# Keeping x transposed through a two-layer hybrid encoder: model dimension on partitions

## The reference

```python
h = rms_norm(x, norm_mix[l])                 # x * rsqrt(mean(x*x) + eps) * gain
proj = h @ w_in[l]                           # 2048 -> 4096, split among four mixers
ya, yb, yc, yd = fourier_mix(..), s5_mix(..), attention_mix(..), rwkv7_mix(..)   # 512 wide each
ycat = rms_norm(stack(ya, yb, yc, yd), branch_norm[l])
x = x + ycat @ w_out[l]                      # 2048 -> 2048
x = x + peer_ffn(rms_norm(x, norm_ffn[l]), peer_w_query[l], peer_sub_keys[l], peer_u[l], peer_v[l])
```

## Time and profile before

| | |
|---|---|
| median of 3 executions | 4031.67 us (4027.1 to 4036.65) |
| the profiled execution | 4039.34 us, its span 4037.5 us |
| mean granted PE clock | 0.971 |
| PE busy | 3754.7 us (93%) |
| PEld busy | 3402.6 us (84%) |
| DVE busy | 2310.8 us (57%) |
| ACT busy | 429.9 us (11%) |
| bytes moved | 1077.47 MB, 267 GB/s over the span |

### The profile page before, as it was taken

One profiled execution on the slowest core, in us unless ns is written; L12 is line 12 of the kernel. 1 busy time (PEld: TensorE's weight loads), 2 busy tenths in 40 slices (PEclk: granted clock), 3 DMA queues, 4 the chain that ended last, 5 costly groups with the idle time before them and its releaser, 6 DMA issues. The chain is left out here.

```text
span 4037.5 us, 63918 instructions
## 1 busy us (share of the span) xinstructions
PE 3754.7 (93%) x26660; PEld 3402.6 (84%) x26660; DVE 2310.8 (57%) x4099; ACT 429.9 (11%) x1020; POOL 977.3 (24%) x868
## 2 busy tenths in 40 slices
PE   6997889999999999999869978899999999999997
PEld 5776774899999999999857867748999999999997
DVE  6975752695287534344469757527952875444444
ACT  1013220100111000000010132101001110000000
POOL 2510000034033333333226100000340333333331
PEclk9998899999999999999989988999999999999999
DMA  5340014399799999999744300153997999999997
GB/s 155 117 133 10 1 43 155 123 358 402 277 381 381 414 416 414 415 412 415 317 127 132 118 10 1 43 161 126 369 409 282 380 386 412 415 415 415 412 414 305
DMA packets 334771, 1077.47 MB, mean 267 GB/s; under 512 B 52197, under 2 KB 150873, under 8 KB 268441
## 3 DMA queue, kind: packets, MB, share of 16 engines
q1 hardware_dynamic: 223896, 670.72, 43.8%
q0 software_dynamic: 110592, 402.70, 25.2%
HBM read 1071.23 MB, written 2.10 MB: 266 GB/s over the span
## 5 line engine op out<-in xcount | busy, mean ns | idle before, releaser
L1745 PE MATMUL bank<-ex_W,ex_tile 128*128 128x160 f32 x8192 | 1132.6, 300 | 39.1 <-DMA ex_tile<-in_peer_v 38.8
L1745 PEld LDWEIGHTS bank<-ex_W,ex_tile 128*128 128x128 f32 x8192 | 1114.9, 190 | 60.3 <-DMA ex_tile<-in_peer_v 52.9
L1672 PE MATMUL bank<-ycT,ex_tile 128*128 128x160 f32 x8192 | 1142.8, 300 | 24.0 <-DMA ex_tile<-in_peer_uT 21.7
L1672 PEld LDWEIGHTS bank<-ycT,ex_tile 128*128 128x128 f32 x8192 | 1119.3, 190 | 39.9 <-DMA ex_tile<-in_peer_uT 30.5
L1629 POOL DMA_INDIRECT ex_row<-in_peer_u,ex_rows x384 | 404.1, 1052 | 1850.9 <-DVE ex_rows L1905 1188.7
L1941 DVE SCALAR_TENSOR_TENSOR ex_sums<-ex_row,ex_weight,ex_sums 128x2048 f32<-128x2048 f32 x186 | 437.0, 2349 | 411.4 <-DMA ex_row<-in_peer_v,ex_rows 362.3
L1935 DVE CUSTOM_DVE_ANT_0 ex_row<-ex_row,ex_h_wide 128x2048 f32<-128x2048 f32 x192 | 438.7, 2290 | 366.7 <-DMA ex_row<-in_peer_u,ex_rows 288.9
L1629 POOL DMA_INDIRECT ex_row<-in_peer_v,ex_rows x384 | 364.7, 950 | 890.2 <-DVE ex_sums L1941 560.5
L359 PE MATMUL pj_bank<-pj_hT,pj_piece 128*128 128x256 f32 x2048 | 459.5, 383 | 5.9 <-DVE pj_hT L632 3.6
L359 PEld LDWEIGHTS pj_bank<-pj_hT,pj_piece 128*128 128x128 f32 x2048 | 388.4, 192 | 72.0 <-issue 13.8
L824 PE MATMUL bank<-arena,ycT 128*128 128x512 f32 x512 | 222.4, 593 | 2.0 <-PEq L909 2.0
(11 more groups left out here) (375 smaller groups left out, 3129.3 us busy)
## 6 DMA issues: line engine op xcount, KB each, us to landing
ex_tile<-in_peer_uT SPq DMA_DIRECT2D x256, 1024.0 KB
ex_tile<-in_peer_v SPq DMA_DIRECT2D x256, 1024.0 KB
pj_piece<-in_w_in SPq DMA_DIRECT2D x32, 2048.0 KB, 8.8
arena<-in_w_out SPq DMA_DIRECT2D x16, 2048.0 KB, 8.2
query_w<-in_peer_w_query SPq DMA_DIRECT2D x16, 1024.0 KB, 6.0
ex_row<-in_peer_u,ex_rows POOLq DMA_INDIRECT x384
ex_row<-in_peer_v,ex_rows POOLq DMA_INDIRECT x384
x<-in_x SPq DMA_DIRECT2D x1, 2048.0 KB, 8.8
```

What stands on the lines that cost most here:

```text
L1672: mm = mmul(o, ring[:, j % SLOTS, k * P:k * P + P], hT[k // 4][:, k % 4, 0:DENSE], start=(k == 0), stop=(k == KT - 1))
L1745: mm = mmul(bank[:, at_, lo:lo + DENSE], ring[:, i % SLOTS, m * P:m * P + P], W[:, j, :], start=(j == 0 and m % 3 == 0), stop=(j == TILES ...
```

## The change

x stays `[P, KT, SEQ]`, dimension on partitions, from the input to the output; the host hands it in transposed and transposes the result.

- Front of mixers: ACT squares x in four quarters; PE multiplies them with a matrix of ones (16 calls of 256 columns into one bank), which leaves each token's sum on every partition; ACT takes the root of 128x256, DVE inverts it and forms hT with 16 products of x, gain and 1/rms. No transposes of h. s5_w_glu has a place of its own. PE waits for hT tile by tile in the first two parts.
- Output projection: w_out is the weight and ycT streams: 32 calls of 256 columns a piece.
- route: no turns. hT is x times gain from SBUF, after the last piece; squares of all 16 tiles are kept and summed by 16 calls with ones, 12 ahead of the 12 query calls and 4 behind them; root and reciprocal are 128x256; PE turns two tiles of it for the column that the scores need.
- experts: hT is scaled by the wide 1/rms from SBUF. A fold is 16 calls with the sums as weights and the 0/1 matrix streaming 32 columns, and one add. At the end DVE adds the six banks straight to x, then the fold of set 2; no copies, no turns back.

The diff, cut to its core:

```diff
-        x = sb(whole, "x", [P, TB, D])
+        x = sb(whole, "x", [P, KT, SEQ])
...
-                for b in range(TB):
...
-                    pe.wait_ge(h_ready, b + 1)
-                    for k in range(KT):
-                        if b == 1 and k == 12:
-                            pe.wait_ge(cols_ready, 2)
-                        mm = tr(bank[:, 4 * b + k // 4, k % 4 * P:k % 4 * P + P], h[:, k * P:k * P + P], c("ident"))
-                        if k % 4 == 3:
-                            mm.then_inc(hT_mm, 1)
-                pe.wait_ge(hT_ready, 8)
+                for q in range(4):
+                    pe.wait_ge(sq_x, q + 1)
+                    for m in range(4):
+                        mm = mmul(bank[:, 4, 0:SEQ], c("ones"), work[:, q, m * SEQ:m * SEQ + SEQ], start=(q == 0 and m == 0),
+                                  stop=(q == 3 and m == 3))
+                mm.then_inc(sums_mm, 1)
...
+                            if part < 2:
+                                pe.wait_ge(hT_ready, k + 1)
...
-                for b in range(TB):
-                    do(A.activation(work[:, 0:2, :].rearrange("p a n -> p (a n)"), x[:, b, :], ACT.Square,
-                                    accum_out=ssq[:, b:b + 1]))
-                    do(A.activation(ssq[:, 2 + b:3 + b], ssq[:, b:b + 1], ACT.Sqrt, scale=1.0 / D, bias=c("eps")), rms_ready)
+                for q in range(4):
+                    do(A.activation(work[:, q, :].rearrange("p (k s) -> p k s", k=4), x[:, 4 * q:4 * q + 4, :], ACT.Square),
+                       sq_x, wait=False)
+                act.wait_ge(sums_mm, 1)
+                do(A.activation(rstd[:], bank[:, 4, 0:SEQ], ACT.Sqrt, scale=1.0 / D, bias=c("eps")), rms_ready)
...
-                for b in range(TB):
-                    dve.wait_ge(rms_ready, b + 1)
-                    do(V.reciprocal(ssq[:, 4 + b:5 + b], ssq[:, 2 + b:3 + b]))
-                    if b:
-                        dve.wait_ge(hT_mm, 4)
-                    do(V.tensor_scalar(h[:], x[:, b, :], ssq[:, 4 + b:5 + b], None, ALU.mult), h_ready)
...
-                for b in range(TB):
-                    for q in range(4):
-                        dve.wait_ge(hT_mm, 4 * b + q + 1)
-                        do(V.tensor_tensor(hT[:, 4 * q:4 * q + 4, b * P:b * P + P],
-                                           bank[:, 4 * b + q, :].rearrange("p (k s) -> p k s", k=4),
-                                           col("norm_mix", 4 * q, 4).unsqueeze(2).to_broadcast([P, 4, P]), ALU.mult),
-                           hT_ready, wait=False)
+                dve.wait_ge(rms_ready, 1)
+                do(V.reciprocal(rstd[:], rstd[:]), rstd_ready)
+                for k in range(KT):
+                    do(V.scalar_tensor_tensor(hT[:, k, :], x[:, k, :], col("norm_mix", k), rstd[:], ALU.mult, ALU.mult),
+                       hT_ready, wait=False)
...
-        b, k = divmod(j, HALF_K)
-        mm = nc.tensor.matmul(bank[:, out_bank(n) + b, :], ycT[:, kh * HALF_K + k, b * P:b * P + P], out_w["place"][:, i % 2, k, :],
-                              start=(kh == 0 and k == 0), stop=(kh == 1 and k == HALF_K - 1), skip_group_check=True)
-    if last == TB * HALF_K:
+        m, k = divmod(j, HALF_K)
+        mm = nc.tensor.matmul(bank[:, out_bank(n) + m // 2, m % 2 * SEQ:m % 2 * SEQ + SEQ],
+                              out_w["place"][:, i % 2, k, m * P:m * P + P], ycT[:, kh * HALF_K + k, :],
+                              start=(kh == 0 and k == 0 and m % 2 == 0), stop=(kh == 1 and k == HALF_K - 1),
+                              skip_group_check=True)
...
+                tr, mmul = nc.tensor.transpose, nc.tensor.matmul
+
+                def sums(first, last):
+                    for k in range(first, last):
+                        if k % 2 == 0:
+                            pe.wait_ge(squared, k // 2 + 1)
+                        mm = mmul(bank[:, 7, 0:SEQ], c("ones"), squares[:, k, :], start=(k == 0), stop=(k == KT - 1),
+                                  skip_group_check=True)
+                    if last == KT:
+                        mm.then_inc(sums_mm, 1)

                 for i in range(EARLY, len(OUT_PIECES)):
                     if i == len(OUT_PIECES) - 2:
-
...
-                    if i == len(OUT_PIECES) - 1:
-                        pe.wait_ge(sk_out, 2)
-                        turn(0)
-                        turn(1)
-                    out_products(nc, out_w, bank, pe, ycT, i, 0, TB * HALF_K)
-                turn(2)
+                    out_products(nc, out_w, bank, pe, ycT, i, 0, OUT_MM)
+                pe.wait_ge(sk_out, 2)
+                sums(0, 12)
                 pe.wait_ge(query["w_in"][0], 16)
-                pe.wait_ge(hT_ready, 2)
-                query_products(nc, query, bank, hT, 0, 0, 8)
-                turn(3)
                 pe.wait_ge(hT_ready, 3)
-                query_products(nc, query, bank, hT, 0, 8, 12)
+                query_products(nc, query, bank, hT, 0, 0, 12)
+                sums(12, KT)
+                pe.wait_ge(rstd_ready, 1)
+                for b in range(TB):
+                    mm = tr(bank[:, 6, b * P:b * P + P], rstd[:, b * P:b * P + P], c("ident"))
+                mm.then_inc(rms_mm, 1)
...
+                    for e in range(2):
+                        act.wait_ge(x_added, 2 * g + e + 1)
+                        two = slice(4 * g + 2 * e, 4 * g + 2 * e + 2)
+                        do(A.activation(squares[:, two, :], x[:, two, :], ACT.Square), squared, wait=False)
+                act.wait_ge(sums_mm, 1)
+                do(A.activation(root[:], bank[:, 7, 0:SEQ], ACT.Sqrt, scale=1.0 / D, bias=c("eps")), root_ready)

...
-
-                def turned(g):
-                    dve.wait_ge(turn_mm, g + 1)
-                    a = 6 if g == 3 else out_bank(g)
-                    do(V.tensor_tensor(hT[g].rearrange("p k (b s) -> p b k s", b=TB),
-                                       bank[:, a:a + 2, :].rearrange("p b (k s) -> p b k s", k=4),
-                                       col("norm_ffn", 4 * g, 4).unsqueeze(1).unsqueeze(3).to_broadcast([P, TB, 4, P]),
-                                       ALU.mult), hT_ready)
-
                 for g in range(4):
-                    if g == 3:
-                        turned(0)
-                        turned(1)
                     dve.wait_ge(out_w["used"], 5 + g)
-                    for b in range(TB):
-                        xs = x[:, b, g * GW:(g + 1) * GW]
-                        do(V.tensor_tensor(xs, bank[:, out_bank(g) + b, :], xs, ALU.add), x_added)
-                turned(2)
-                turned(3)
-                dve.wait_ge(sums_ready, 8)
-                do(V.tensor_reduce(rms[:, 0], ssq[:], AX.X, ALU.add), sum_ready)
-                dve.wait_ge(rms_ready, 1)
-                do(V.reciprocal(rms[:, 2], rms[:, 1]))
+                    for e in range(2):
+                        xs = x[:, 4 * g + 2 * e:4 * g + 2 * e + 2, :].rearrange("p k s -> p (k s)")
+                        do(V.tensor_tensor(xs, bank[:, out_bank(g) + e, :], xs, ALU.add), x_added)
+                    if g < 3:
+                        continue
+                    for q in range(4):
+                        do(V.tensor_tensor(hT[q], x[:, 4 * q:4 * q + 4, :],
+                                           col("norm_ffn", 4 * q, 4).unsqueeze(2).to_broadcast([P, 4, SEQ]), ALU.mult),
+                           hT_ready, wait=False)
+                dve.wait_ge(root_ready, 1)
+                do(V.reciprocal(rstd[:], root[:]), rstd_ready)
+                dve.wait_ge(rms_mm, 1)
+                do(V.tensor_copy(rms[:], bank[:, 6, 0:SEQ].rearrange("p (b s) -> p b s", b=TB)[:, :, 0]), rms_ready)
+                dve.wait_ge(hT_ready, 4)
...
+                def fold(s):

                     pe.wait_ge(sums_ready, s + 1)
...
-                    mmul(bank[r, 6 + n % 2, :], c("fold"), sums[:, n * GW:n * GW + GW], start=True, stop=True)\
-                        .then_inc(fold_mm, 1)
+                    pe.wait_ge(*((wide_out, 8), (wide_out, 12), (fold_added, 2))[s])
+                    for m in range(KT):
+                        mm = mmul(bank[:, 6, m * SET:m * SET + SET], sums[:, m * P:m * P + P], c("fold"), start=(m == 0),
+                                  stop=True, skip_group_check=True)
+                    mm.then_inc(fold_mm, 1)
...
-                for n in range(4):
-                    fold(2, n)
-                for n in range(2 * 4):
-                    g, b = divmod(n, 2)
-                    count = min(P, DENSE - b * P)
-                    pe.wait_ge(out_out, max((4 * g + 3) // 3, n % 6 if n < 6 else 0) + 1)
-                    if n >= 6:
-                        pe.wait_ge(x_added, n - 5)
-                    for k in range(4):
-                        mm = tr(bank[0:count, OUT_BANKS[n % 6], k * P:k * P + P], outT[:, 4 * g + k, b * P:b * P + count],
-                                c("ident"))
```

(31 more changed lines are left out.)

136 lines of the change are left out of this document (50 added, 86 removed).

## The result

The changed kernel takes 4050.85 us in the median of five executions (4046.88 to 4055.5), the kernel before 4033.73 (4027.1 to 4036.65): a ratio of 1.0045, interval 1.0031 to 1.0059. By the medians it is slower by 17 us, 0.42%; I had forecast 4037, no change, with a range to 4046. Run once more beside other kernels, it gave 1.0050 (1.0036 to 1.0063). The ratios are estimates from all executions with a 95% interval; they differ by up to 0.0008 from the quotients of the medians.

The account below looks back on a forecast made before the run. DMA was taken to bound only each layer's second half, PE the 58 us after experts' start. Terms gave +2.35 us a layer, +4.7 for two, +5.2 with the store: 4037 us, own range 4031 to 4040, with rivals 4026 to 4046.

Parts of the forecast that it names:

- The chain behind the last piece: End of route, last w_out piece to first product of experts: products with ones, root, reciprocal, two transposes; +8.3 us a layer.
- The transposes' -0.2: Start of experts: the two transposes of the widened norm go, -0.2 us a layer.
- The w_out stage: Output projection: 256 calls of 256 columns cost +0.8 us, 16 transposes before the last piece go, -1.75 us, per layer.
- The end: Layer's end, after the last tile: six adds from PSUM and a fold, no copies or transposes; -4.8 us, bounds -5 and -2.4.
- The store: Output written in rows of 1 KB and not 8 KB: +0.5 us, bounds 0 and +1.6.
- The restart's clock: PE's clock at the start of experts, after waiting for root and reciprocal; no loss from it in the sum.
- rival (a): Start of experts: clock at 1.2 GHz after PE's idle gaps, 1.7 to 3.4 us lost a layer; chance 0.27.
- The front at 0: First norm of each layer: cost 0, since PE must wait for the S5 tables' transfer anyway.
- only lateness can count: Front: the S5 table transfer, its place in SP's queue unchanged, cuts the front off, so only work later than it costs.
- the bound of +4: Front, upper bound for both layers: all products with ones at half clock, S5 chain late by 2.9 and about 1 us.
- The S5 argument chain: VectorE work behind hT in layer 0's front: ending near 38.3 against the table transfer at 39.70, 1.4 us to spare.
- Folds 0 and 1 at 0: Folds in the tiles' stretch: 32 records take 3.8 us against 3.80, at one place and not four; no change.

Follow-up runs that it names:

- The pair of runs on the kernel before: Kernel before with sixteen added 32-column products at folds 0 and 1: in one lump 4052.98 us, ratio 1.0051; four ahead of each quarter 4040.46 us, ratio 1.0026.

## Why the prediction was wrong

The table leaves 11.2 us that I did not have (16.4 and not 5.2): the way to the first tile +5.3, the fronts +3.7, tiles +2.3, mixers and rwkv +2.1, less 1.7 at the ends and 0.6 in w_out.

**What held.** The chain behind the last piece: +8.0 against +8.3. The transposes' -0.2. The w_out stage: -1.23 a layer against -0.95, so the products cost +0.5 and not +0.8. The end: -5.7 against -4.8, since the six adds from PSUM take 3.15 us and begin as the last tile ends (2007.22). The store: 7.91 us from issue to the span's end in both traces of after, 7.65 and 7.40 in those of before, +0.4 for my +0.5. None of these misses is worth 1 us over both layers but the end's, which was 1.7 us better than I said.

**The restart's clock** is the first step that failed. I costed the query products behind the border at 1.97 us, at full clock, and kept the fall as rival (a), 1.7 to 3.4 us a layer, chance 0.27. It came true in both layers: 1.7 and 4.2 us, 5.9 together, the second above the rival's own bound. Even with it the forecast would have been at most 4043.8, so this step alone does not make the miss. My reading was that the gap of 2.30 us in layer 1's front did no harm and the one of 3.55 did; mine was drawn as 2.7 and 0.9 with two transposes between, measured 2.35 and 0.79, and the clock fell. The length of a gap does not settle it: my own rows have a gap of 2.99 us with the clock full behind it, which I read only as a wait. The page "TensorE: Matmul & The Clock Gate" of the Trainium skill (Why this matters for your kernels) warns of idle gaps between bursts of products. Here the clock did drop behind such gaps, though both were shorter than those that the page warns of, and it did not behind the 2.99 us. The fall does not always last longer in layer 1: the stretch of 78.4 us is in layer 1 in both traces of after, in layer 0 with the C tables moved, and in neither layer (75.7 to 75.8) with x in one row or with the folds spread.

**The front at 0** is the second. The argument that only lateness can count was right, and so was the bound of +4; it came to +2.7 and +1.0. The S5 argument chain, which I followed, was not late: it ended at 39.1 and the table's step came at 43.48. What was late was the queue in which the table stands. I had priced short rows for x (bounds 0 and +1.6) only for the store, not for the load at the head of that queue: SP waits for x to land, and 1.1 to 1.2 us go to every issue behind it in layer 0. The load of `s5_c_re` then takes some 2.9 us to issue for 2.2, in both layers; why is open. My 4 us was the price of another mechanism, products with ones at half clock and a late S5 chain, so that the bound held is luck; its own terms (24 more records at 0.43 and not 0.22 us, less 1.4 us to spare) give about 3.7 and not 2.9 us for layer 0.

**Folds 0 and 1 at 0** is the third, by its reason: "3.8 us against 3.80 now, at one place and not at four. No change". The duration was right (3.65), and the place was what mattered. In one lump the narrow products bring the clock down behind them; spread, they don't. The pair of runs on the kernel before shows it: 12.5 us for the lump itself by the medians, 8.4 by the traces. On after, it is 6.5 us in tiles and ends by the traces. Against before the table shows only +2.3 for the tiles. The new fold may be the better one apart from its lump: spread, it gives stretches of 1207.1 and 1205.5 us, where the second trace of before has 1207.8 and 1210.1. That it is, and by what (one add on DVE in place of four, or something else), no run shows.

**Open in part** are the +2.1 us in mixers and rwkv, where the two layers of one trace differ by up to 3.4 us (the run with the root early). Over all traces, ten such stretches of kernels with before's front and w_out average 555.7 us and eighteen with after's 556.3. The clock behind PE's wait for the S5 tables goes some way to explain it: it is down there in 8 of the 18 and in none of the 10; the 8 average 557.6 us, the other ten 555.3. Three of the four stretches of after itself are among the 8. That this is the cause is argued from the traces; no run kept PE busy there.

## What to carry to other kernels

When a reduction over a wide tile replaces one over a column, follow its tail: root and reciprocal of 128x256 take 2.2 us that a column hid, and here the engine that waited for them restarted at half clock, which cost another 1.7 to 4.2 us. Put the last contribution as early as its data allow, and keep independent products for behind it. A queue of issues is a path too: what is late at its head is late for all behind it. And work that is equal in duration is not equal in kind: here narrow products did no harm in fours between wide ones, and did in a lump of sixteen.

## What the runs showed of the hardware

The granted clock fell to 0.5 (1.2 GHz) behind busy PE: 32 records of 128-column weights with 32 streaming columns, 3.65 us back to back, were followed by a stretch at that level, between 3 and 7 us long, in 15 of 24 such folds in six traces of after and its edits and in four of four on the kernel before; in none of 16 parts of four products in each of four kernels. Of the 24, fold 0, which in all these traces follows a tile without a gap, has it in 5 of 12, and fold 1, mostly behind a gap of 0.7 to 1.0 us, in 10 of 12. Whether it is the few streaming columns, the many weight loads or the number of records in a row that does it, no run separates.

A gap of 2.35 us, two transposes and a gap of 0.79 lowered the clock in ten of ten places; one of 0.79 alone did not. The length of a single gap does not decide: behind PE's wait for the S5 tables the clock fell after gaps of 2.17 to 3.33 us in 8 places and stayed full after ten others of 1.70 to 3.35 us there, among them the 2.99 of the earlier trace rows. The 2.30 of the earlier trace rows, at another place, did not lower it either. Before fold 2, gaps of 1.61 and 2.41 us with the 32 narrow records behind them gave 5.98 and 6.39 us for 3.73, but there the lump itself may be the cause.

In the stretch that transfers fill, a few microseconds of half clock are not hidden: the DMA share went to 0.64 behind them, and the next issue of a tile came 12.3 us after the last and not 4.35.
